# Order of attention and boundary work, and a 4 + 9 panel pool in place of 5 + 8, in a three-layer transformer kernel

## The reference

```python
for layer in range(2):                      # first block
    y = rmsnorm(h, norm_g[layer, 0])
    y = gmlp_mixer(...) if layer == 0 else diff_attention(...)   # 8 heads, two score maps each, T5 bias
    h = h + rmsnorm(y, norm_g[layer, 1])
    h = h + rmsnorm(conv_ffn(rmsnorm(h, norm_g[layer, 2])), norm_g[layer, 3])   # 1024 -> 2 x 2816 -> 1024
# second block
x = x + 0.5 * swiglu(rms_norm(x, ffn1_norm))
u = rms_norm(x, mix_norm) @ w_in            # MLA (8 heads, low-rank q and kv, rope) and MoBA (8 heads, ALiBi)
x = x + concat(mla, moba) @ w_out
x = x + 0.5 * swiglu(rms_norm(x, ffn2_norm))
return rms_norm(x, final_norm)
```

## Time and profile before

| | us |
|---|---|
| median of 3 runs | 1098.09 (1097.35 to 1098.18) |
| the profiled execution, own time | 1100.18 |
| its span, first to last instruction | 1098.4 |
| PE busy | 1065.8 (97%) |
| DVE busy | 783.5 (71%) |
| ACT busy | 647.0 (59%) |
| DMA moved | 197.62 MB, mean 180 GB/s |

### The profile page before, as it was taken

One profiled execution on the slowest core, in us unless ns is written; L12 is line 12 of the kernel. 1 busy time (PEld: TensorE's weight loads), 2 busy tenths in 40 slices (PEclk: granted clock), 3 DMA queues, 4 the chain that ended last, 5 costly groups with the idle time before them and its releaser, 6 DMA issues.

```text
span 1098.4 us, 15623 instructions
## 1 busy us (share of the span) xinstructions
PE 1065.8 (97%) x5956; PEld 919.4 (84%) x5956; DVE 783.5 (71%) x1253; ACT 647.0 (59%) x1152; POOL 37.8 (3%) x39
## 2 busy tenths in 40 slices
PE   7999999999999899999999999999999989999997
PEld 5888888887898778888887888888899878888886
DVE  5888988788667989878877756656666847556555
ACT  6667665666647777566566545445455647455443
POOL 0830000000000000000000000000000000000000
PEclk9999999999999999999999999999999989999999
DMA  9765765655562346565554665666443515555551
GB/s 358 245 201 152 236 194 188 201 183 190 182 202 82 114 149 234 189 200 184 191 174 143 225 200 178 192 197 206 138 154 113 192 58 164 197 195 176 197 183 39
DMA packets 56250, 197.62 MB, mean 180 GB/s; under 512 B 6560, under 2 KB 8008, under 8 KB 56176
## 3 DMA queue, kind: packets, MB, share of 16 engines
q1 hardware_dynamic: 55920, 196.42, 54.4%
q0 software_dynamic: 112, 0.20, 0.1%
q10 hardware_dynamic: 144, 0.00, 0.0%
HBM read 195.35 MB, written 1.25 MB: 179 GB/s over the span
## 4 chain that ended last, share of the span: by engine, by line
PE 81%; DVE 11%; ACT 5%; issue 1%; DMA 1%; SPq 0%; ACTq 0%; DVEq 0%
PE G L1380 25%; PE Y L1424 23%; PE G L1384 13%; DVE w_low L828 4%; PE G L1401 2%; PE G L1402 2%; PE G L1407 2%; PE G L1365 2%; PE G L1366 2%; PE G L1367 2%; PE Y L1419 2%; ACT w_high L439 1%; DVE w L957 1%; DMA raw<-in_panels 1%; PE G L1543 1%
## 5 line engine op out<-in xcount | busy, mean ns | idle before, releaser
L828 DVE TENSOR_TENSOR w_low<-raw,w_high 128x1024 fp32r<-128x1024 f32 x352 | 423.5, 1222 | 44.6 <-ACT w_high L439 43.1
L439 ACT CAST w_high<-raw 128x1024 fp32r<-128x1024 f32 x352 | 362.8, 1046 | 18.2 <-DMA raw<-in_panels 10.5
L1380 PE MATMUL G<-x_parts,w_high 128*128 128x512 f32 x1280 | 319.7, 392 | 1.6 <-DVE w L930 1.6
L1380 PEld LDWEIGHTS G<-x_parts,w_high 128*128 128x128 f32 x1280 | 234.1, 188 | 46.7 <-DVE w L930 2.0
L522 ACT COPY big<-G 128x512 f32<-128x512 f32 x80 | 46.9, 586 | 239.6 <-PE G L1384 239.6
L1384 PEld LDWEIGHTS G<-x_parts,w_low 128*128 128x128 f32 x1280 | 174.6, 190 | 12.5
L1384 PE MATMUL G<-x_parts,w_low 128*128 128x256 f32 x1280 | 178.5, 282 | 0.0
L930 DVE TENSOR_TENSOR w<-G,big 128x512 f32<-128x512 f32 x80 | 55.3, 691 | 166.2 <-ACT big L522 166.0
L1424 PE MATMUL Y<-w_high,a_high 128*128 128x512 f32 x420 | 132.5, 397 | 1.5 <-DVE a_low L1186 1.1
L1424 PE MATMUL Y<-w_high,a_low 128*128 128x512 f32 x420 | 130.4, 392 | 0.0
L1424 PE MATMUL Y<-w_low,a_high 128*128 128x512 f32 x420 | 130.1, 391 | 0.0
(11 more groups left out here) (241 smaller groups left out, 1195.1 us busy)
## 6 DMA issues: line engine op xcount, KB each, us to landing
raw<-in_panels SPq DMA_DIRECT2D x352, 512.0 KB, 4.4
gain_pre<-in_gains SPq DMA_DIRECT2D x7, 512.0 KB, 5.5
gain_post<-in_gains SPq DMA_DIRECT2D x4, 512.0 KB, 6.5
big<-in_xT SPq DMA_DIRECT2D x4, 256.0 KB, 7.3
h<-in_x SPq DMA_DIRECT2D x2, 512.0 KB, 8.7
big<-rel_rows SPq DMA_DIRECT2D x8, 128.0 KB, 5.2
out_y<-w SPq DMA_DIRECT2D x4, 256.0 KB, 2.2
big<-in_w_s SPq DMA_DIRECT2D x1, 512.0 KB, 10.0
```

The source lines that it names most:

```text
L439: s.copy(WH[:, n % RING, :], raw[:, n % RAWS, :]).then_inc(hi, 1)
L828: v.tensor_tensor(WL[:, n % RING, :], raw[:, n % RAWS, :], WH[:, n % RING, :].bitcast(F32), ALU.subtract).then_inc(lo, 1)
L1380: mm(out, WH[:, n % RING, k * P:(k + 1) * P], X2[:, k, :, :], start=k == 0, stop=False, skip_group_check=True)
```

## The change

Five things are changed.

1. **The pool.** `RAWS` 5 to 4, `RING` 8 to 9. The buffer for one panel more in the ring is also paid by laying `lamrow`, `posi` and `posb` over other tiles.
2. **The boundary.** A stage ends with panel base + 1 of the next split, not base + 2; base + 2 follows the normed x of t = 0, and base + 3 its turned x.
3. **Diff attention.** q and k are copied out by ACT (`qk_out`), and the order of splits, exponentials, squares and combining is another in every step; `scores(6)` and `scores(7)` come earlier in step 7; the t = 1 rows of the first tail panel stand before the fourth.
4. **The latents' rms.** DVE adds the squares first (`csum`), one matmul of 512 columns with `ones` gives the sums on all partitions, ACT takes two roots of 128 x 256 and DVE two reciprocals; `column_factors`, its wait and the diagonals are gone.
5. **MIX.** `exps(a + 1)` stands before the split, not after it, `out_rows(3)` comes before `turn(15, 0)`, and the tail has four panels.

```diff
-RAWS = 5
-RING = 8
+RAWS = 4
+RING = 9
@@ scalar: boundary
                     y_square(b, 0, 0), y_square(b, 0, 1)
                     y_root(b, 0)
-                    upto(base + 3)
+                    upto(base + 2)
                 h_rms(b, 0)
-                if b not in POST:
-                    upto(base + 3)
+                upto(base + 2)
                 x_high(b, 0, 0), x_high(b, 0, 1)
+                upto(base + 3)
                 if b in POST:
                     y_square(b, 1, 0)
@@ scalar and vector: ffn
-                upto(base + 3 * NF + 2)
+                upto(base + 3 * NF + 1)
@@ vector: boundary
                 half_mean(b, 0)
-                if b in POST:
-                    upto(STARTS[b] + 3)
                 x_normed(b, 0)
+                upto(STARTS[b] + 2)
                 x_low(b, 0, 0), x_low(b, 0, 1)
                 if b in POST:
                     y_gained(b, 1, 0)
                     y_half_mean(b, 1)
                     x_low(b, 0, 2)
+                    upto(STARTS[b] + 3)
                     y_gained(b, 1, 1)
                     h_add(b, 1)
@@ scalar: diff attention
+            def qk_out(k):
+                act.wait_ge(used, DIFF + 10 + 2 * k)
+                s.activation(qk[:, k % 2, 0, :], G[:, k % 2, 0:T], ACT.Copy, scale=DIFF_D ** -0.5)
+                s.copy(qk[:, k % 2, 1, :], G[:, k % 2, T:2 * T]).then_inc(qk_r, 1)
+
             for k in range(HEADS):
                 if k >= 2:
                     turned_out(k - 2, 0)
+                qk_out(k)
...
@@ vector: diff attention
             for k in range(HEADS):
-                evac_qk(k, DIFF + 10 + 2 * k, DIFF_D ** -0.5)
-                if k == 6:
-                    low_head(0)
-                elif k < 5:
-                    upto(DIFF + 15 + 2 * k)
                 if k >= 1:
                     combine(k - 1)
...
+                if k >= 2:
+                    head_values(k - 2)
...
+                elif k < 7:
+                    upto(DIFF + (15 + 2 * k if k < 5 else 26))
+                if 1 <= k < 7:
+                    weigh(k - 1)
+                if k < 5:
+                    upto(DIFF + 16 + 2 * k)
...
@@ tensor: tail
-                for i in range(last):
+                for i in range(last + 1):
+                    if i == first_at:
+                        part(0, 1)
                     part(i, 0)
-                part(0, 1)
-                part(last, 0)
@@ tensor: diff attention, step 7 and tail
                         head_out(2)
+                        scores(6)
...
-                if k >= 1:
+                if 1 <= k < 7:
                     scores(k - 1)
...
                     head_rows(0, 0)
+                    scores(7)
...
-                  (4, 0): lambda: head_split(7)})
+                  (4, 0): lambda: head_split(7)}, 3)
@@ MIX: the latents' rms
+            link(v.tensor_tensor(csum, csq[:, 0:4:3, :], csq[:, 1:5:3, :], ALU.add))
+            v.tensor_tensor(csum[:, 0, :], csum[:, 0, :], csq[:, 2, :], ALU.add).then_inc(csum_r, 1)
...
+            s.activation(cstd_q, Z[:, 0:T], ACT.Sqrt, bias=eps[:], scale=1.0 / Q_RANK)
+            s.activation(cstd_kv, Z[:, T:2 * T], ACT.Sqrt, bias=eps[:], scale=1.0 / KV_RANK)
...
-            dve.wait_ge(cbc, 1)
-            v.tensor_tensor(CR, facq[:], PB[:, 0:T], ALU.mult)
-            v.tensor_copy(rkv[0:64, :], PB[0:64, T:2 * T]).then_inc(cb_r, 1)
-            dve.wait_ge(cb_r, 1)
             weigh(8)
+            v.reciprocal(rkv[0:64, :], cstd_kv[0:64, :])
+            link(v.reciprocal(CR, cstd_q))
+            link(v.tensor_tensor(CR, CR, facq[:], ALU.mult))
             upto(B + 17)
...
-                pe.wait_ge(csq_r, 3)
+                pe.wait_ge(csum_r, 1)
+                mm(Z[:, 0:2 * T], ones[:], csum[:].rearrange("p a t -> p (a t)"), start=True, stop=True)
                 for t in range(TT):
-                    for c0, ks in ((4, range(3)), (6, range(3, 5))):
-                        for k in ks:
...
+                    last = mm(Y[:, 2, t:t + 1], csum[:, 1, tok(t)], ones[:, 0:1], start=True, stop=True)
...
             moba_pair(1)
-            column_factors()
-            pe.wait_ge(cb_r, 1)
@@ MIX: exponentials, output rows, tail
             for a in range(12, 16):
                 turned_out(a, 0), turned_out(a, 1)
                 if a > 12:
                     cast(a - 1)
-                upto(B + min(20 + a, 34))
                 if a < 15:
                     exps(a + 1)
+                upto(B + min(20 + a, 34))
...
+            out_rows(3)
             turn(15, 0), turn(15, 1)
...
-            tail(6, [(k + 4) % KT for k in range(3, 8)], True,
+            tail(6, [(k + 4) % KT for k in range(4, 8)], True,
```

More of the change, by code:

```diff
@@ L126, in build_program @@
         ones = sb("ones", [P, P])
-        diag = sb("diag", [P, 4, P])
-        rtc = sb("rtc", [P, 4])
-        stdc = sb("stdc", [P, 4])
+        diag = sb("diag", [P, TT, P])
+        rtc = sb("rtc", [P, TT])
+        stdc = sb("stdc", [P, TT])
         eps = sb("eps", [P, 1])
@@ L177, in build_program @@
         CR, rkv = CRs[:], rkvs[:]
+        csum = big2[:, 0:2 * T].rearrange("p (a t) -> p a t", a=2)
+        cstd_q, cstd_kv = (big2[:, (2 + i) * T:(3 + i) * T] for i in range(2))
         relw = otk[:].rearrange("p a b c -> p (a b c)")[0:32, 0:HEADS + REL]
@@ L736, in _ @@
             turned_out(7, 0)
-            high_head(3)
-            upto(DIFF + 30)
-            high_head(4)
+            high_head(3), high_head(4)
+            upto(DIFF + 29)
             squares_out(7).then_inc(ac, 1)
             rms_out(7, HEADS, 4)
+            high_head(5)
             upto(DIFF + 31)
-            for e in range(5, HEADS):
+            for e in range(6, HEADS):
                 high_head(e)
-                upto(DIFF + 27 + e)
+                upto(DIFF + 26 + e)
+            upto(DIFF + 34)
             boundary(3, ACT.Gelu_apprx_tanh)
@@ L788, in _ @@
             cast(9)
+            exps(11)
             upto(B + 22)
-            exps(11)
             turned_out(11, 0), turned_out(11, 1)
@@ L799, in _ @@
             for t in range(TT):
-                s.activation(mlaV[:, t, :], G[:, 1 - t, :], ACT.Copy, scale=rtc[:, 2 + t:3 + t]).then_inc(mlav_r, 1)
+                s.activation(mlaV[:, t, :], G[:, 1 - t, :], ACT.Copy, scale=rtc[:, t:t + 1]).then_inc(mlav_r, 1)
             upto(B + 31)
@@ L1222, in _ @@
             norm_head(6)
-            low_head(3)
+            low_head(3), low_head(4)
             head_values(7)
-            low_head(4)
-            upto(DIFF + 30)
+            upto(DIFF + 29)
+            low_head(5)
             inverse_rms(7, HEADS, 4)
             norm_head(7)
+            upto(DIFF + 30)
+            low_head(6)
             upto(DIFF + 31)
-            for e in range(5, HEADS):
-                low_head(e)
-                upto(DIFF + 27 + e)
+            low_head(7)
+            upto(DIFF + 34)
             boundary(3)
@@ L1260, in _ @@
             dve.wait_ge(cstd, 1)
-            link(v.reciprocal(rtc[:], stdc[:]))
-            for t in range(4):
-                last = v.tensor_scalar(diag[:, t, :], ident, rtc[:, t:t + 1], None, ALU.mult)
-            last.then_inc(cdiag, 1)
+            v.reciprocal(rtc[:], stdc[:])
             dve.wait_ge(tab_r, 1)
@@ L1322, in _ @@
             weigh(11)
+            upto(B + 22)
             queries(1)
@@ L1433, in turn_x, with tail @@
                 last.then_inc(xt_r, 1)
-            def tail(b, slots, early, hooks=None):
+            def tail(b, slots, early, hooks=None, first_at=None):
                 hooks = hooks or {}
                 last = len(slots) - 1
+                if first_at is None:
+                    first_at = last
                 def part(i, t):
@@ L1692, in column_sums @@
                 mm(Y[:, 3, 0:T], cst[:, K_PERM:K_PERM + P], krt[:], start=True, stop=True).then_inc(kr_ps, 1)
-            def column_factors():
-                pe.wait_ge(cdiag, 1)
-                for t in range(4):
-                    last = mm(PB[:, t * P:(t + 1) * P], ones[:], diag[:, t, :], start=True, stop=True)
-                last.then_inc(cbc, 1)
             def moba_pair(j):
```

96 lines of the change are left out of this document (45 added, 51 removed).

## The result

| | before | after |
|---|---|---|
| median | 1098.13 (4 runs, 1097.35 to 1098.50) | 1108.05 (4 runs, 1105.53 to 1110.96) |
| the profiled execution, own time and span | 1100.18, 1098.4 | 1110.96, 1109.2 |
| PE, DVE, ACT busy | 1065.8, 783.5, 647.0 | 1064.6, 784.7, 653.7 |

The ratio after to before is 1.0088, 95% interval 1.0067 to 1.0108: 0.9% slower. The forecast was 1094.1, range 1087 to 1101. It has the wrong sign, and the time lies 7 us above its range.

The account below looks back on a forecast made before the run. The prediction took PE, 97% busy, plus its few waits to bound the kernel. Savings of 18.85 us less losses of 14.85 left 4.0 us off, a median of 1094.1 us, range 1087 to 1101.

Parts of the forecast that it names:

- The four FFN starts: First summed tile of each FFN: five casts, not four, before the second activation; 7.15 us lost, bounds 0 and 15.
- Clock: New waits at boundary t = 1 and FFN starts could lower PE's clock: 1.3 us lost, bounds 0 and 5.
- MIX + 30: This panel's load waits for split 26, its cast delays the MLA value copies: 2.3 us lost, bounds 1 and 3.5.
- The raw pool in steady work: Steady FFN work: the ring of nine makes up for the missing raw buffer, nothing lost.
- Boundaries 1 and 3: Moving base + 3 behind the first normed x delays that of t = 1: 4.1 us lost, 2.05 each.
- Boundaries 2 and 4: The wait for the normed x at t = 0 and the slow clock go: 4.7 us saved.
- Diff attention: Combining starts earlier, ACT copies q and k, and stalls of PE go: 5.1 us saved, bounds 3.5 and 6.
- Latents and MoBA: New sums of squares replace one-column passes and diagonals, at the price of two reciprocals: 3.95 us saved.
- End of MIX: Moved output rows and earlier exponentials fill PE's wait, clock stays up: 5.1 us saved, bounds 2.7 and 5.7.
- The raw pool decides: Rival: late loads at FFN starts and MIX + 30 cost 10 us more than counted: 1104 us; chance 0.13.
- The clock eats the gain: Rival: PE restarts at 0.50 after idling at boundaries 1 to 4 and two FFN starts: 1098.5, no change; chance 0.14.
- The reciprocals were long: Rival: the latents' reciprocals take 2 us each and step 9 of MIX waits: 1095.6 us; chance 0.10.

Follow-up runs that it names:

- e1: The changed kernel with five raw and eight split buffers, its new orders kept; 1093.77 us, ratio 0.9950.
- e2: The kernel before with four raw and nine split buffers, all its old orders kept; 1113.96 us, ratio 1.0134.
- e7: The kernel before with four raw buffers, not five, the ring still eight; 1107.98 us, ratio 1.0080.
- e11: The kernel before with four raw and nine split buffers, ACT and DVE taking one panel fewer within an FFN's first two tiles; 1103.44 us, ratio 1.0050.
- e5: The changed kernel with five raw and eight split buffers, and boundaries 1 and 3 in their old order; 1087.80 us, ratio 0.9901.
- e8: The kernel before with only the boundaries, and the last panel ahead of them, in their new order; 1102.39 us, ratio 1.0032.
- e9: As e5, with scaled outputs of MIX pairs 12 to 15 ahead of the split and two long reciprocals moved into holes of DVE; 1083.18 us, ratio 0.9860.
- e10: As e9, with six raw and eight split buffers; 1081.53 us, ratio 0.9845.

## Why the prediction was wrong

The forecast had 14.75 us saved by the orders (18.85 less 4.1 at boundaries 1 and 3) and 10.7 lost to the pool and the clock. The runs have 5.0 saved (e1) and 15.2 lost (e2; 14.3 with the new orders). So both sums failed, the savings by 9.8 and the losses by 4.5 or 3.6, and together they are the error of 14. With the orders as forecast the change would have come out near even. The steps that failed are, on the side of the losses, the size of the four FFN starts (7.15 us, 10.5 in e2) and the clock behind them (left at nothing, 6.2 in e2). On the side of the savings they are boundaries 1 and 3 (4.1 lost, 5.3 in e1's trace), boundaries 2 and 4 (4.7, 2.7 in e1) and the end of MIX (5.1, 3.3 in e1).

*The four FFN starts, 7.15 us.* The mechanism was right and every mark of it is in the trace: five casts, loads at the pace of the splits, PE at the first summed tile. The size was not: 10.5 us in e2. FFN1 and FFN3 came as forecast (2.7 and 2.2, forecast 2.65 and 2.3). FFN0 was put at 0.7 "(its landings are already spread out)" and cost 2.9, and FFN2 at 1.5 and cost 2.7. The sentence on FFN0 took the landings for independent of each other. In the changed kernel's chain, PE's wait at 118.23 leads back to its own end at 105.06:

```profile
105.09 1.06 ACT w_high L441
106.15 0.02 issue
106.17 1.24 DVE w_low L841
107.41 0.02 issue
107.42 5.66 DMA raw<-in_panels
...
113.16 1.05 ACT w_high L441
114.20 0.32 ACT w L558
```

A cast needs a split buffer that PE frees, its split frees the raw buffer that the panel four later needs, and only then does that load go out. Spread-out landings are the sign of this loop, not slack.

*Clock, 1.3 us.* In e2 the stretches behind the four starts lose 6.2 us. I had left them at nothing with "where a stall on DVE follows, it hides"; in e2 none did. In the changed kernel it was so at FFN0 and FFN1 (2.8 and 1.6 us), while FFN2 and FFN3 went on at 1.00. At boundaries 1 and 3 it is part of the 6.0 below. Starts, clock and MIX + 30 are 19.0 us in e2's trace, far over the forecast; boundaries 2 and 4 give 4.9 back there.

*MIX + 30, 2.3 us.* Right: 2.26 in e2, and PE waits there for the copies of the MLA values, 2.1 us. In the changed kernel and in e7 the slow clock behind it takes 1.4 more.

*The raw pool in steady work, 0.* Right, and with less than I thought was needed. From the third pair of wide tiles to the last of each FFN the lag against the kernel before changes by 0.01 us or less in the changed kernel, in e2, and in e7, which has no ninth buffer. So in this work nothing has to make up for the raw buffer; the 4.5 us that the ninth buffer gives in e11 stand at boundaries 2 and 4.

*Boundaries 1 and 3, 4.1 us lost.* e5 gives 6.0 between the medians and 3.7, up to FFN2, between the profiled executions. The waits are as forecast, 2.27 and 2.09 us against 2.05 each. Behind them the clock took 0.9 and 1.6 in e1, and FFN0's start takes up 1.3 of what boundary 1 loses; neither was counted. That the rest of the 6.0 is clock too, in the executions without a profile, is not shown.

*Boundaries 2 and 4, 4.7 us saved.* In e1 1.1 and 1.6, and the same in e8. The wait at t = 0 did not go, as the walk had it, but shrank from 2.0 to 0.63 and 0.65 us; the slow clock behind it is gone; and t = 1 got one of 1.10 and 1.14, near the forecast 1.4. The gain is 2.7 in sum, inside the bounds and 2.0 short.

*Diff attention, 5.1 us.* 4.8 in e1: four times 0.6 to 0.7 in the first steps, then 0.4 in two, then 1.7. In the tail the 1.13 us of the low head are gone, but at boundary 3 the normed x of t = 0 is later than the shorter tail wants it (PE waits 0.85 us in e1 and 1.07 in e5, and did not before). Not forecast.

*Latents and MoBA, 3.95 us.* At pair 8 the lag falls by 4.3 us in e1. Three waits at pairs 8 to 10, about 0.6 us each as lost time, give back 1.8, and `exps(11)` brings 0.57: 3.1. One of them was forecast, the 0.65 at head 10, but it was left out of the sum: 0.85, 0.9, 0.84 and 1.2 less 0.35 are 3.4 without it. The reciprocals took 1.71 and 1.68 us for 256 columns, 6.6 ns a column, not the 1.2 that I chose between 0.4 and 2.0. The slope of the earlier trace rows, 7.3 ns, was right within 10%. The rule of the Trainium skill, "VectorE: DVE Perf Modes", section "Walkthrough: the 8-slice pipeline in each mode", had led to an estimate of 2.1 us; the trace agrees that a column costs many times what it costs a copy (0.42 us for the same width) and is 20% below the estimate. I had two pointers to a long reciprocal and took the middle.

*End of MIX, 5.1 us.* 3.3 in e1, from pair 12 to boundary 6, and 5.3 in e9. The first term counted the 2.75 us of the moved work, where the wait to be filled was 2.55. What was missing above all is DVE: I moved ACT's casts behind the exponentials and did not move what stands behind them, the split that waits for the cast and the scaled outputs behind the split. That cost 2.1 us of waits, and one edit took it back. In the changed kernel a slow clock came on top, at 0.50 from 899.3 to 902.6 us; e1, with the same waits, had 1.00 there.

*What is not placed.* The savings read at the landmarks of e1 come to 9.1 us between the two profiled executions, to 5.0 between the medians. The terms above place the 5.6 us between 14.75 and 9.1: boundaries 1 and 3 1.2 (5.3 lost in e1), boundaries 2 and 4 2.0, diff attention 0.3, the latents 0.9 and the end of MIX 1.8, less 0.5 by which e1's first stage happened to be faster. The profile of before was 1.4 us above the median of its 17 runs, that of e1 2.7 below its own. The spread goes with the clock: of those 17 runs the eight fastest have a mean granted clock of 0.993 or 0.994 and the nine slowest 0.990 to 0.992, and e9 and e10, whose profiles have no slow stretch before the last 6 us, spread over 0.8 and 0.5 us where the kernel before spreads over 4. Which stretches the other executions had is not on record. In e8, whose sums of the latents are the old ones, the clock behind them was 1.00, where the kernel before had 0.50. So the other 4 us of the 9.8 lie between single executions and medians, and this part stays open; I had counted the slow stretches of one profile as certain.

*The rivals.* "The raw pool decides", at 0.13, came nearest: its turning point, 1 us a start above my 1.8, was nearly met at the starts (2.6 in e2) and passed with their clock (4.2). But it gives 1104 with all savings as forecast, and two thirds of the error lie in them, so that it is not the whole of what happened. "The clock eats the gain" named boundaries 1 to 4 and two starts; in the changed kernel it was boundary 1, two starts and two places in MIX, in e1 boundaries 1 and 3. The reciprocals were long as well. These three are independent and of one sign, and I had priced them as alternatives. Two of the rivals' sums are also a little off: 1094.1 and 4.8 are 1098.9, and 1098.1 less 12.5 is 1085.6.

## What to carry to other kernels

A pool of buffers between a load and its use is a loop: divide the round trip (here 6.9 us from issue to next issue) by the number of buffers, and compare it with the burst's demand, not with the mean. When a ring gets one slot more, look at where the fixed order of an engine puts the extra fill: here a cast that nobody needed yet stood ahead of an activation that PE awaited, and cost 10.5 us. When instructions are moved behind others on one engine, walk the second engine's queue as well, from the instruction that waits for the moved one to the next that somebody else awaits.

## What the runs showed of the hardware

- TensorE's clock after a wait is not set by the length of the wait alone. It was 0.54 behind 2.26 us at 94.59 us and 1.00 behind the same 2.26 at 404.66, both in e8, with the same kinds of matmuls behind. In e1 the wait at 398.77 (2.09 us) was followed by 3.3 us at 0.50. The changed kernel's starts of FFN2 and FFN3 waited 2.36 and 3.03 us and went on at 1.00, while those of FFN0 and FFN1, with 4.37 and 3.76, went on at about half. At 898.55 us two waits of 0.66 and 0.81 us were followed by 0.50 in the changed kernel, and the same two by 1.00 in e1. Windows of the changed kernel, columns as above:

```profile
619.80:624.00 4.20, 4.17 (x22) 3.61 (x23) 3.62 (x5) 3.11 (x7) 0.00 (x0) 1.00 0.46 152
941.80:946.00 4.20, 4.18 (x22) 3.63 (x23) 3.63 (x5) 3.11 (x7) 0.00 (x0) 1.00 0.41 123
```

- RECIPROCAL on DVE took 1.68 to 1.75 us for 256 columns, and as long on 64 partitions as on 128 (1.71 and 1.68 us). A copy of the same width took 0.42.
